# Hybrid attention encoder on one core: rows 0 to 3 of the norm between the layers planned over eighteen steps in place of sixteen

## What is computed

```python
def rms_norm(x, g):
    y = x32 * lax.rsqrt(jnp.mean(x32 * x32, axis=-1, keepdims=True) + EPS)
    return (y * g).astype(x.dtype)

for l in range(DEPTH):                       # DEPTH = 2
    h = rms_norm(x, pre_norm_g[l])
    if l % 2 == 0:                           # A: differential attention; B: window of 2 chunks, sinks
        proj = h @ w_in_ab
        y = concat([ya * silu(ga), yb * silu(gb)]) @ w_out_ab
    else:                                    # C: attention over 9 chunks of 64 with a position bias
        proj = h @ w_in_c
        y = (yc * silu(gc)) @ w_out_c
    x = x + rms_norm(y, post_norm_g[l])
```

## Time and profile before

| | |
|---|---|
| median of three runs | 1233.83 us (1233.18 to 1234.98) |
| the profiled execution | 1234.73 us, span 1232.9 us |
| PE | 1190.8 us busy, 97% |
| DVE | 805.4 us, 65% |
| ACT | 588.5 us, 48% |
| POOL | 431.4 us, 35% |
| mean granted clock of PE | 0.992 |

### The profile page before, as it was taken

One profiled execution on the slowest core, in us unless ns is written; L12 is line 12 of the kernel. 1 busy time (PEld: TensorE's weight loads), 2 busy tenths in 40 slices (PEclk: granted clock), 3 DMA queues, 4 the chain that ended last, 5 costly groups with the idle time before them and its releaser, 6 DMA issues.

```text
span 1232.9 us, 17663 instructions
## 1 busy us (share of the span) xinstructions
PE 1190.8 (97%) x6496; PEld 1013.7 (82%) x6496; DVE 805.4 (65%) x1707; ACT 588.5 (48%) x1296; POOL 431.4 (35%) x556
## 2 busy tenths in 40 slices
PE   7999999999999999898999999999999999999986
PEld 6988888888888887686888888888888888888874
DVE  4574765757767668867544866848658576585675
ACT  5554443434444556654454544435434444354453
POOL 5333214133173465564752114124141241412312
PEclk9999999999999999999999999999999999999988
DMA  5161201011022153253121102011020110201025
GB/s 193 49 210 35 69 18 52 18 52 35 18 86 63 41 154 103 69 149 130 57 70 53 48 18 73 18 56 52 18 73 18 56 52 18 73 18 56 25 56 108
DMA packets 93703, 78.95 MB, mean 64 GB/s; under 512 B 3089, under 2 KB 83985, under 8 KB 93618
## 3 DMA queue, kind: packets, MB, share of 16 engines
q1 hardware_dynamic: 92754, 74.68, 19.8%
q0 software_dynamic: 864, 3.15, 1.7%
HBM read 69.38 MB, written 13.68 MB: 67 GB/s over the span
## 4 chain that ended last, share of the span: by engine, by line
PE 48%; DVE 2%; ACT 1%; POOL 1%; issue 1%; DVEq 0%; ACTq 0%; POOLq 0%
PE dense L1128 25%; PE dense L1136 7%; PE pv_ps L1255 6%; PE scores L1335 4%; PE turned L1302 4%; PE turned L1290 1%; DVE pT_lo L1832 0%; DVE e_sb L1767 0%; ACT k_hh L1436 0%; POOL w_lo L980 0%; POOL rowstat L1006 0%; PE scores L1136 0%; DVE o_sb L1882 0%; DVE fin L2011 0%; ACT junk L1616 0%
## 5 line engine op out<-in xcount | busy, mean ns | idle before, releaser
L1128 PE MATMUL dense<-hT_hi,w_hi 128*128 128x512 f32 x880 | 350.9, 399 | 0.0
L1128 PE MATMUL dense<-hT_lo,w_hi 128*128 128x512 f32 x880 | 344.9, 392 | 0.0
L1128 PE MATMUL dense<-hT_hi,w_lo 128*128 128x512 f32 x880 | 344.5, 391 | 0.0
L973 POOL TENSOR_SCALAR w_hi<-w_f 128x1024 fp32r<-128x1024 f32 x86 | 93.2, 1084 | 645.6 <-PE dense L1128 588.9
L980 POOL TENSOR_TENSOR w_lo<-w_f,w_hi 128x256 fp32r<-128x256 f32 x344 | 264.3, 799 | 7.2
L1443 ACT ACTIVATE e_sb<-e_sb,low 128x256 f32<-128x256 f32 (+7 forms) x256 | 170.3, 665 | 172.3 <-DVE low L1767 170.1
L1476 ACT ACTIVATE pT_hi<-turned 128x640 fp32r<-128x640 f32 (+3 forms) x224 | 117.2, 523 | 167.9 <-PE pv_ps L1255 94.2
L1128 PEld LDWEIGHTS dense<-hT_hi,w_lo 128*128 128x128 f32 x880 | 165.6, 188 | 36.8
L1128 PEld LDWEIGHTS dense<-hT_hi,w_hi 128*128 128x128 f32 x880 | 166.1, 189 | 26.0 <-issue 0.3
L1128 PEld LDWEIGHTS dense<-hT_lo,w_hi 128*128 128x128 f32 x880 | 166.3, 189 | 25.2
L1767 DVE CUSTOM_DVE_ANT_0 e_sb<-scores,bias 128x640 f32<-128x640 f32 (+3 forms) x192 | 131.5, 686 | 44.1 <-PE scores L1335 42.1
(11 more groups left out here) (215 smaller groups left out, 1809.8 us busy)
## 6 DMA issues: line engine op xcount, KB each, us to landing
w_f<-in_w_in_c SPq DMA_DIRECT2D x37, 512.0 KB, 4.1
w_f<-in_w_in_ab SPq DMA_DIRECT2D x34, 512.0 KB, 3.9
rel_tiles_dram<-rel_rows_dram SPq DMA_DIRECT2D x1, 5120.0 KB, 22.9
bias<-rel_tiles_dram SPq DMA_DIRECT2D x8, 640.0 KB, 5.4
y<-in_x SPq DMA_DIRECT2D x8, 512.0 KB, 7.7
hT_lo_f<-in_x SPq DMA_DIRECT2D x8, 512.0 KB, 7.0
out_x<-y SPq DMA_DIRECT2D x8, 512.0 KB, 3.8
w_f<-in_w_out_c SPq DMA_DIRECT2D x8, 512.0 KB, 3.8
```

Of the source, the lines that this page charges most:

```text
L973: ts(hi, src, 1.0, 1.0, ALU.mult, ALU.mult).then_inc(w_hi_done, 1)
L1128: last = mm(dense[:, x.n % 2, :], lhs[:, d * P:(d + 1) * P], rhs[:, d, x.f * HALF:(x.f + 1) * HALF], start=i == 0, stop=i == 23)
```

## The change

Three tables of steps change; no operation is added, removed or altered in itself. Steps before and after, for rows 0 to 3 (second number of turn: its second half):

| row | ysq | yg | x1 | xsq | scaled | turn |
|---|---|---|---|---|---|---|
| 0 | 117 | 118 | 119 | 120 | 122 -> 123 | 124, 125 -> 125, 126 |
| 1 | 119 | 120 -> 121 | 121 -> 122 | 122 -> 124 | 124 -> 126 | 126, 127 -> 128, 129 |
| 2 | 121 | 123 -> 124 | 125 | 126 -> 127 | 128 -> 129 | 129, 130 -> 130, 133 |
| 3 | 123 | 126 -> 127 | 127 -> 128 | 128 -> 130 | 130 -> 132 | 133, 134 -> 134, 135 |

The eight output products of (B4, B5) stood in steps 131, 132, 135 to 140, and stand in 131, 132, 136 to 141. With the last of them the load of the gate weights of C0 goes from step 140 to 141 and their split from 142 to 143.

```diff
-OUT_STEPS = {0: (3, 4, 6, 7, 8, 9, 11, 12), 2: (3, 4, 5, 6, 7, 8, 9, 10), 4: (3, 4, 7, 8, 9, 10, 11, 12)}
+OUT_STEPS = {0: (3, 4, 6, 7, 8, 9, 11, 12), 2: (3, 4, 5, 6, 7, 8, 9, 10), 4: (3, 4, 8, 9, 10, 11, 12, 13)}
...
-NORM = [Row(0, *b_steps(4.5, 4.6, 4.7, 5.0, 5.2, 5.4)), Row(1, *b_steps(4.7, 5.0, 5.1, 5.2, 5.4, 5.6)),
-        Row(2, *b_steps(5.1, 5.3, 5.5, 5.6, 6.0, 6.1)), Row(3, *b_steps(5.3, 5.6, 5.7, 6.0, 6.2, 6.5))]
+NORM = [Row(0, *b_steps(4.5, 4.6, 4.7, 5.0, 5.3, 5.5)), Row(1, *b_steps(4.7, 5.1, 5.2, 5.4, 5.6, 6.0)),
+        Row(2, *b_steps(5.1, 5.4, 5.5, 5.7, 6.1, 6.2)), Row(3, *b_steps(5.3, 5.7, 6.0, 6.2, 6.4, 6.6))]
...
-for n_, late_ in zip(NORM[:4], b_steps(5.5, 5.7, 6.2, 6.6)):
+for n_, late_ in zip(NORM[:4], b_steps(5.6, 6.1, 6.5, 6.7)):
```

## The result

The changed kernel takes **1237.35 us** in the median of eight runs (1233.02 to 1238.32); beside it the kernel before takes 1233.47 us, also of eight (1231.99 to 1234.98). The ratio is 1.0026, with a 95% interval of 1.0015 to 1.0037. A second set of nine runs gives 1237.03 us and 1.0024 (1.0014 to 1.0033). So the change costs 3.6 to 3.9 us where the sum said +0.65. Two slow executions in the experiments, one of `after_row3_early` (1981.15 us) and one of `after_half_pieces` (2397.08 us), are left out of all medians and ratios.

The account below looks back on a forecast made before the run. PE was taken to bound the kernel (97% busy), with DVE binding some 25 us. Terms -0.97 + 1.2 + 0.43 = +0.65 us moved the median from 1233.83 to 1234.5 us, range 1231.2 to 1237.0 (8 in 10).

Parts of the forecast that it names:

- the sum: Whole kernel: -0.97 us at the output product, +1.2 for `scaled` of row 3, +0.43 for a half turn, giving +0.65 us.
- Steps 120 and 121: `times g_post` of row 1 leaves step 120, so PE wins about 0.5 us there.
- The path of DVE from step 124 to 130: From the `q_st` drain to step 130's first drain: 20.86 + 0.52 - 1.4 = 20.0 us.
- I keep them; their bounds are 0 and 3.1 us: About 2.1 us by which DVE operations in steps 124 to 130 ran longer beside POOL's splits, kept unchanged.
- Where PE stalls: No stall at step 125; 2.5 to 3 us at 126, none at 127, about 2.5 us at 129.
- Step 131: ACT's square of row 3 (1.05 us) stands ahead of `hT_hi`; the output product starts at 510.1, 0.97 us won.
- Steps 132 and 133: `scaled` of row 3 (1.2 us) stands ahead of the output drain: a stall of about 1.4 us, formerly 0.2.
- POOL and SP: Step 124's split starts near 487.7, four splits stay hidden until about 509; C0's gate load lands 1 to 4 us later.
- The POOL delays shrink: Rival, chance 0.14: the 2.1 us of DVE delays fall near zero as POOL starts later; -1.5 us, 1232.3 us.
- the third rival: Chance 0.15: PE's clock falls after stalls of some 2.9 us at steps 126 and 129; 1.7 us each, 1236.2 to 1237.9.
- Late splits: Rival, chance 0.06: POOL's four splits take 5 us each, PE waits up to 3 us in step 132; 1237 or more.
- vanishing stalls: Rival, chance 0.08: spreading the rows wins half or more of PE's 7.0 us of waits; 1230.3 us or less.

Follow-up runs that it names:

- after_row3_early: Changed kernel, but for row 3 the square of x1 in step 129 (not 130) and `scaled` in 131 (not 132): 1234.55 us, 1.0007.
- after_half_pieces: Changed kernel with four POOL weight splits cut into eight subtractions of 128x128 each, in place of four of 128x256: 1233.87 us, 1.0000.
- the three piece sizes: Changed kernel with POOL's four weight splits in pieces of 128x128, 128x256 (as it stands) or 128x512: 1233.87, 1237.35 and 1238.41 us.
- with fills: Kernel before and changed kernel, both with the subtractions of four POOL weight splits replaced by one memset each: 1230.28 and 1232.20 us.
- after_memset: Changed kernel with the subtractions of four POOL weight splits replaced by one memset each: 1232.20 us, 0.9987.
- rows23_only: Kernel before with only rows 2 and 3 and the output products moved as in the change, rows 0 and 1 as before: 1236.42 us, 1.0032.

## Why the prediction was wrong in size and right in place

The median came out at 1237.35 where 1234.5 was said, outside the range by 0.35 us, and 3.9 us above the kernel before, more than the 2.5 us that the prediction counted as no change. By its own steps:

- **Steps 120 and 121: held.** From the square of row 0 to the start of `q_st` on DVE took 486.28 - 461.60 = 24.68 us before and 483.51 - 459.37 = 24.14 after: 0.54 us won, as said.
- **The path of DVE from step 124 to 130: here it failed.** The sum had 20.0 us, 22.90 were measured. Its count of operations was right: with the lengthening measured, 20.0 - 2.1 + 5.1 = 23.0. The term that was mis-sized is "I keep them; their bounds are 0 and 3.1 us". That term was priced as a total carried over from before, not as something that each operation meets anew. The text had the rule in hand that gives the other number: the Trainium skill, "SBUF — State Buffer", section "SBUF: two separate sides", has VectorE and GpSimd hold their shared ports for a whole instruction each. The trace agrees, by the table of the three piece sizes above. By it, with POOL working almost without a gap from 485 to 508 (which the prediction also said), about nine operations of the path at 0.4 to 0.5 us each come to 4 us or more, as the x1 of 1.76 us and the `scaled` of 1.58 already let one guess. I wrote the rule down and let the sum stay.
- **Where PE stalls: held.** None at 125, 3.24 at 126 (2.5 to 3 said), 4.07 at 129 (2.5 said; between the drain that ended the stall of 126, at 489.75, and that of 501.36 four operations were 2.2 us longer than usual in sum).
- **Step 131: held.** From the first drain of step 130 to the output product 4.34 us (510.75 - 506.41); the prediction's numbers give 510.1 - 505.75 = 4.35. ACT's rows are those foretold, answering to the earlier trace rows:

```profile
508.22 1.04 ACT L1626 ACTIVATE junk<-y 128x1024 bf16<-128x1024 f32 x1
...
509.38 0.60 ACT L1528 ACTIVATE hT_hi<-dense 128x512 fp32r<-128x512 f32 x1
```

- **Steps 132 and 133: held.** `scaled` took 1.28 us ahead of the drain (1.2 said), and the stall was 1.38 (1.4 said):

```profile
517.72 1.28 DVE L2001 SCALAR_TENSOR_TENSOR hT_lo_f<-y,rowstat,g_pre 128x1024 f32<-128x1024 f32 x1
519.04 0.69 DVE L1731 TENSOR_TENSOR y<-dense,y 128x512 f32<-128x512 f32 x1
```

- **POOL and SP: held.** The split of step 124 began at 485.41, which is 487.6 when put beside the trace of before (485.41 + 461.60 - 459.37); 487.7 was said. Four splits ended at 507.8 and no fill waited for one. The gate load of C0 is behind the loads of x now, and POOL waits 4.83 us for it at 556.53; no engine waits for that split.
- **The whole.** Predicted +0.65, and 2.9 us more on the path of DVE, make 3.55; the stretch has 3.66. From the other side: the same two orders at equal lengthening differ by 92.76 - 91.86 = 0.90 us (half pieces against before, 2.2 and 2.1 us) or, with fills, by 0.50. The +0.65 lies between.
- **The rivals.** "The POOL delays shrink" had the right term and the wrong sign: the delays grew by as much as it let them fall. The clock fell, as the third rival had it; it was named as a sign of being wrong, but the waits behind hid it, as the text took it to. The length of a stall, which that rival made its condition, doesn't decide: the clock stayed at 1.00 behind 3.24 us in the first execution and fell behind 2.30 us in `after_memset`. Late splits and vanishing stalls didn't come.

What stays open: the rows give POOL's four pieces as one line, so which piece met which operation is read from times that overlap, not shown one by one. One row doesn't fit to the last tenth: a `den` at 486.94 took its usual 0.15 us although the copy beside it is recorded until 487.08. And the 0.50 to 0.90 us that the order costs by itself were split off only for row 3, and there for two terms together. The stretch of each variant is that of one execution; only the changed kernel has two, 0.03 us apart.

## What to carry to other kernels

A delay that one engine does to another is not a sum to be carried over: count the operations of the new order that will meet a running instruction of the other engine, and price each at some two thirds of that instruction's length (0.46 to 0.61 us here for pieces of 0.7). Where such operations stand ahead of a drain that PE waits for, a smaller instruction on the other engine can be worth more than the order (2.8 us of the stretch here, where the order by itself cost 0.5 to 0.9), but the long ones left among them can still be met. And compare stretches between fixed operations, not spans: here one execution's luck outside the stretch was as large as the effect in it.

## What the runs showed of the hardware that was not expected

- An operation of DVE with two SBUF inputs waited for POOL's running instruction even where its own work was tiny: `den`, 0.15 us alone, took 1.04 beside a copy of 1.05 us. Over pieces of 128, 256 and 512 columns the same x1 took 1.47, 1.74 and 2.28 us against 1.28 alone. Drains with one input in PSUM stayed at 0.68 us in all three.
- The clock of PE went from 1.00 to 0.50, that is 1.2 GHz, after a stall of 4.07 us in one execution; in another of the same kernel, windows after stalls of 3.24 and 2.78 us had 0.69 and 0.59. The stretch was 95.52 and 95.55 us. Where PE had another wait ahead of it, its slowness cost nothing; where it had none, in `rows23_only`, it cost 1.3 us.
- How long the stall was didn't decide whether the clock fell: 2.30 us were followed by 0.50 in `after_memset`, 3.24 us by 1.00 in the first execution of the changed kernel.
- An operation with two SBUF inputs that began beside a fill on POOL (0.95 us) was not lengthened: gating 0.39, x1 1.28 us.
